# Differential heads: the gate's second part goes behind the context's row tiles, and the last row tile is turned beside it

## Chip, cores and metric

The kernel runs on one core of one Trainium2 chip. Times are microseconds of device time. TensorE (PE) multiplies and transposes, VectorE (DVE) and ScalarE (ACT) read its results, GpSimd (POOL) prepares the weights, and SyncE (SP) issues the weight loads.

## What is computed

The reference is two transformer blocks on 512 tokens. The change lies in the first layer of the second block, differential attention with eight heads over 512 tokens (four tiles of 128) and 256 context tokens (two tiles):

```python
q, k, v, z = project(h)          # and the same for the context, hc
q = apply_rope(q, cos, sin); k = apply_rope(k, cos, sin)   # tokens only
k_all = concat([k, kc]); v_all = concat([v, vc])
o1 = sweep_attention(qq[..., 0, :], kk[..., 0, :], vv)     # one softmax per half head
o2 = sweep_attention(qq[..., 1, :], kk[..., 1, :], vv)
o = rms_norm(o1 - lam * o2, subln_g) * (1 - lam_init)
return (o * silu(gate)) @ w_out
```

All of it is fp32 to the accuracy of a split: a weight `w` is kept as `w_hi` and `w_lo`, the activations likewise, and each product is three matmuls (hi by hi, lo by hi, hi by lo).

## The kernel before, in words

Each engine has its own instruction stream, written out by hand, and semaphores tie them together. The stages follow one another; `pe_heads`, `act_heads` and `dve_heads` are the stage of the differential heads.

Head `hd` is attended in twelve steps `n` (six query tiles by two half heads; `HEAD_TILES` gives the order). In each, PE makes the scores (`pe_head_scores`, into banks 0 and 1), DVE takes the extreme (`dve_head_least`), ACT the exponential (`act_head_exp`), and later PE transposes the mixed probabilities (`pe_head_at`) and multiplies by the values (`pe_head_values`). Between these steps PE fills its time with projections, in chunks of three matmuls; `HEAD_FILL` says how many chunks behind each step, 62 in all, and what is left over follows the twelfth step (`for _ in beside: pass`).

The units of this filling during head `hd` are listed by `beside_units(hd)`, each of eight chunks: six **row** units of head `hd + 1` (q, k and v of one token tile, 384 columns; tiles 0 to 3 are tokens, 4 and 5 the context) and two **z** units of head `hd` (its gate: z 0 with 512 columns, z 1 with 256). Before, the order is rows 0 to 3, z 0, z 1, row 4, row 5. Head 7 has no rows beside it. The results go into banks 5 and 6 in turn, and a unit waits until the one two before it has been read.

A row tile, once projected, is copied or rotated into `rot` (`act_head_rows` for the context, `dve_head_rows` for tokens), **turned** by four transposes on PE (`pe_head_turn`, bank 7), and read out of the bank by ACT into `q` and `k_hi` (`act_head_turned`, lines 1934 and 1935) and by DVE into `q` and `k_lo` (`dve_head_turned`, lines 2726 and 2727); the last raises `head_ready`. A turn waits for the tile's copy and for `head_ready` of the tile before. Tile `t - 1` is turned behind chunk 6 of unit `t`, tile 3 behind chunk 6 of z 0, and tile 5 at the very end of the head. The first scores of the next head wait for `head_ready` of its tile 5, and for the exponential of step 11.

The weights of head `hd` are one tile of four pairs of chunks. SP loads a pair into one of two raw buffers (four transfers of 128 KB), when POOL has split the pair two before it. POOL splits it (lines 465 and 467) into `w_hi` and `w_lo`, of which there are **two slots**: head `hd + 2` goes into the slot of head `hd`. Ahead of the first pair POOL waits for the last product that reads the slot's old tile. `product_behind` names it, and the diff leaves it as it is:

```python
if what == "head":
    return ("z", tile[1], 1)
```

PE waits for the split of a pair ahead of chunks 0, 2, 4 and 6 of a unit (`split_at`). PE's stream is in order: what stands behind a waiting chunk waits too.

Of the kernel before, what the change touches and what calls it, by code (L numbers as in the profile page):

```python
# [18 lines left out]
TX, TC = S // P, C // P  # L19
TA = TX + TC  # L20
# [455 lines left out]
def three(pe, out, a, b, start, stop):  # L476
    pe.matmul(out, a[0], b[0], start=start, stop=False)  # L477
    pe.matmul(out, a[0], b[1], start=False, stop=False)  # L478
    return pe.matmul(out, a[1], b[0], start=False, stop=stop)  # L479


def split_at(k, tile, c):

    h, v = k.sig["w_split"].at(tile)
    return h, v + c // 2
# [91 lines left out]
LAST_HALVES = {4: (0, 1), 5: (2,), 6: (3,), 7: (4,), 8: (5,), 9: (6,)}  # L577
HEAD_TILES = (0, 1, TX, TX + 1, 2, 3)
HEAD_FILL = (4, (2, 1), 6, (3, 2), 6, (3, 2), 6, (5,), 6, (5,), 6, (3, 2))
TURN_AT = 6  # L580


def head_turns(i):
# [4 lines left out]
def beside_units(hd):  # L588

    rows = [("row", hd + 1, t) for t in range(TA)] if hd < 7 else []  # L590
    return rows[0:TX] + [("z", hd, j) for j in range(2)] + rows[TX:]


def bank_order():
# [7 lines left out]
def head_bank(k, unit):  # L602
    kind, hd, t = unit
    return EARLY[t] if kind == "row" and hd == 0 and t in EARLY else 5 + k.bank_order.index(unit) % 2


def head_read(unit):

    kind, hd, t = unit
    if kind == "row":  # L610
        return [("head_v", (hd, t))] + [("head_roped", (hd, t))] * (t < TX)
    return [("head_z", (hd, t))]
# [9 lines left out]
def z_cols(j):  # L622
    return (slice(0, 512), 512) if j == 0 else (slice(512, T6), T6 - 512)
# [427 lines left out]
def tile_before(hd, t):  # L1051

    if hd == 0:
        i = FIRST_ORDER.index(t)
        return (0, FIRST_ORDER[i - 1]) if i > 0 else None
    return (hd, t - 1) if t > 0 else (hd - 1, FIRST_ORDER[-1] if hd == 1 else TA - 1)
# [35 lines left out]
def pe_head_turn(k, pe, hd, t):  # L1092

    s = k.sig
    pe.wait_ge(*s["head_roped" if t < TX else "head_plain"].at((hd, t)))
    if tile_before(hd, t) is not None:
        pe.wait_ge(*s["head_ready"].at(tile_before(hd, t)))
    for v in range(4):
        x = k.rot[:, v, :, :].rearrange("p a n -> p (a n)")
        m = pe.transpose(k.ps[:, 7, v * P:(v + 1) * P], x, k.ident[:, :])  # L1100
    m.then_inc(*s["head_turned"].up((hd, t)))


def pe_beside(k, pe, hd):

    s = k.sig
    for unit in beside_units(hd):
        kind, h, t = unit
        bank, i = head_bank(k, unit), k.bank_order.index(unit)
        if i >= 2:  # L1110
            for name, event in head_read(k.bank_order[i - 2]):
                pe.wait_ge(*s[name].at(event))
        else:
            pe.wait_ge(*s["turn_lo"].at(("h6", TX - 1, 1)))
        tile = ("head", h)
        for c in range(KD):
            if c % 2 == 0:
                pe.wait_ge(*split_at(k, tile, c))
            if kind == "row":
                m = three(pe, k.ps[:, bank, 0:384], [x[:, c, t * P:(t + 1) * P] for x in k.h6], k.hl(tile, c, 0, 384), c == 0, c == KD - 1)  # L1120
            else:
                cols, n = z_cols(t)
                m = three(pe, k.ps[:, bank, 0:n], k.hl(tile, c, 384, P), [x[:, c, cols] for x in k.h6], c == 0, c == KD - 1)
            if c == KD - 1:
                m.then_inc(*s["prod"].up(unit))
            if c == TURN_AT and kind == "row" and 0 < t != TX:
                pe_head_turn(k, pe, h, t - 1)
            if c == TURN_AT and kind == "z" and t == 0 and h < 7:
                pe_head_turn(k, pe, h + 1, TX - 1)
            yield  # L1130
    if hd < 7:
        pe_head_turn(k, pe, hd + 1, TA - 1)


def pe_head_squares(k, pe, hd):
# [53 lines left out]
def pe_heads(k, pe):  # L1189
# [3 lines left out]
    for hd in range(8):  # L1193
        beside = pe_beside(k, pe, hd)

        def fill(n):
            for _ in range(n):
                next(beside, None)
# [12 lines left out]
        for n in range(12):  # L1211
# [6 lines left out]
            elif late is None:  # L1218
                fill(sum(HEAD_FILL[n]) if n % 2 else HEAD_FILL[n])
            else:  # L1220
                for j in range(len(head_turns(late[1]))):
# [3 lines left out]
                    else:  # L1225
                        fill(HEAD_FILL[n][j])
            if n == 4 and hd > 0:
# [687 lines left out]
def act_head_rows(k, act, hd, t):  # L1915

    s = k.sig
    bank = head_bank(k, ("row", hd, t))
    act.wait_ge(*s["prod"].at(("row", hd, t)))
    if t >= TX:  # L1920
        if tile_before(hd, t) is not None:
            act.wait_ge(*s["head_turned"].at(tile_before(hd, t)))
        x = k.ps[:, bank, 0:256].rearrange("p (v o n) -> p v o n", v=4, o=1)
        act.copy(k.rot[:, :, :, :], x.to_broadcast([P, 4, 2, HD])).then_inc(*s["head_plain"].up((hd, t)))
    if hd >= 2 and t == 0:
        act.wait_ge(*s["head_valued"].at((hd - 2, 2)))
    act.copy(k.v6[:, hd % 2, t, :], k.ps[:, bank, 256:384]).then_inc(*s["head_v"].up((hd, t)))


def act_head_turned(k, act, hd, t):  # L1930
    s, b, cols = k.sig, hd % 2, slice(t * P, (t + 1) * P)
    turned = k.ps[:, 7, :].rearrange("p (v n) -> p v n", v=4)
    act.wait_ge(*s["head_turned"].at((hd, t)))
    act.activation(k.q6[0:HD, b, :, cols], turned[0:HD, 0:2, :], ACT.Copy, scale=-(HD ** -0.5))
    act.activation(k.k6[:, b, :, cols], turned[:, 2:4, :], ACT.Copy, scale=1.0).then_inc(*s["head_hi"].up((hd, t)))


def act_beside(k, act, hd):
    s = k.sig
    for unit in beside_units(hd):  # L1940
        kind, h, t = unit
        bank = head_bank(k, unit)
        for c in range(KD):
            if c == TURN_AT and kind == "row" and 0 < t != TX:
                act_head_turned(k, act, h, t - 1)
            if c == TURN_AT and kind == "z" and t == 0 and h < 7:
                act_head_turned(k, act, h + 1, TX - 1)
            if c < KD - 1:
                yield
        if kind == "row":  # L1950
            act_head_rows(k, act, h, t)
        else:
            cols, n = z_cols(t)
            act.wait_ge(*s["prod"].at(unit))
            if 0 < h < 7 and t == 0:
                act.wait_ge(*s["head_y"].at(h - 1))
            act.activation(k.z(h)[:, cols], k.ps[:, bank, 0:n], ACT.Tanh, scale=0.5).then_inc(*s["head_zth"].up((h, t)))
        yield
    if hd < 7:
        act_head_turned(k, act, hd + 1, TA - 1)  # L1960


def act_head_rstd(k, act, hd):
# [44 lines left out]
def act_heads(k, act):  # L2008
# [11 lines left out]
    for hd in range(8):  # L2020
# [6 lines left out]
        for n in range(12):  # L2027
# [10 lines left out]
            elif n % 2 == 0:  # L2038
                fill(HEAD_FILL[n])
            else:  # L2040
                fill(HEAD_FILL[n][0])
            if late is not None and len(head_turns(late[1])) > 1:
                act_head_at(k, act, *late, 1)
            if n % 2 and hd < 7:
                fill(sum(HEAD_FILL[n][1:]))
            for h in LAST_HALVES.get(n, ()) if hd == 7 else ():
# [675 lines left out]
def dve_head_turned(k, dve, hd, t):  # L2722
    s, b, cols = k.sig, hd % 2, slice(t * P, (t + 1) * P)
    turned = k.ps[:, 7, :].rearrange("p (v n) -> p v n", v=4)
    dve.wait_ge(*s["head_hi"].at((hd, t)))
    dve.scalar_tensor_tensor(k.q6[HD:P, b, :, cols], turned[HD:P, 0:2, :], -(HD ** -0.5), k.q6[0:HD, b, :, cols], ALU.mult, ALU.subtract)  # L2726
    dve.tensor_tensor(k.k6lo[:, b, :, cols], turned[:, 2:4, :], k.k6[:, b, :, cols], ALU.subtract).then_inc(*s["head_ready"].up((hd, t)))  # L2727


def dve_beside(k, dve, hd):  # L2730
    s = k.sig
    for unit in beside_units(hd):
        kind, h, t = unit
        bank = head_bank(k, unit)
        for c in range(KD):
            if c == TURN_AT and kind == "row" and 0 < t != TX:
                dve_head_turned(k, dve, h, t - 1)
            if c == TURN_AT and kind == "z" and t == 0 and h < 7:
                dve_head_turned(k, dve, h + 1, TX - 1)
            if c < KD - 1:  # L2740
                yield
        if kind == "row":
            dve_head_rows(k, dve, h, t)
        else:
            cols, n = z_cols(t)
            dve.wait_ge(*s["head_zth"].at((h, t)))
            dve.scalar_tensor_tensor(k.z(h)[:, cols], k.z(h)[:, cols], 1.0, k.ps[:, bank, 0:n], ALU.add, ALU.mult).then_inc(*s["head_z"].up((h, t)))
        yield
    if hd < 7:
        dve_head_turned(k, dve, hd + 1, TA - 1)  # L2750


def dve_head_least(k, dve, hd, n):
# [35 lines left out]
def dve_heads(k, dve):  # L2789
# [11 lines left out]
    for hd in range(8):  # L2801
# [6 lines left out]
        for n in range(12):  # L2808
# [7 lines left out]
            if hd < 7:  # L2816
                fill(sum(HEAD_FILL[n]) if n % 2 else HEAD_FILL[n])
            elif n in LAST_GATE_READ:
# [253 lines left out]
```

## Time and profile before

| | us |
|---|---|
| median of 3 runs | 1768.13 |
| the three runs | 1768.13, 1769.32, 1758.78 |
| profiled execution | 1757.89 |
| its span on the core | 1756.6 |
| PE busy in the span | 1592.8 (91%) |
| DVE busy | 1105.8 (63%) |
| POOL busy | 627.9 (36%) |
| ACT busy | 624.2 (36%) |

The profile is of one execution. A time in a row counts from the start of its span. A busy PE is not PE at its peak, because matmuls are pipelined and their recorded ends overlap the next start; the distance from one matmul's start to the next start is what it costs. "Idle before" in square brackets is time in which the engine sat still, and behind the arrow stands what released it.

### The profile page before, as it was taken

The numbers are of one execution on the slowest core, as the hardware profiler recorded it, in microseconds if no ns is written. First come the engines' busy times: TensorE is split into PE (matmuls) and PEld (weight loads), VectorE is DVE, ScalarE is ACT, GpSimd is POOL, SyncE is SP. The second block draws the span as 40 slices with busy tenths as digits, with TensorE's granted clock in tenths as the row PEclk, the third lists the DMA queues.
The fourth block names the chain that finished last, engine by engine and source line by source line (L and its number), as shares of the span: only waits on it lengthen the run. The fifth ranks groups of instructions, "written<-read, shape, count | busy, mean of one in ns | idle before, by whom it ended". The sixth has DMA issues, their size and how long they took to land. (4 is left out here: it accounts for less than half of the span.)

```text
span 1756.6 us, 21631 instructions
## 1 busy us (share of the span) xinstructions
PE 1592.8 (91%) x7933; PEld 1316.5 (75%) x7933; DVE 1105.8 (63%) x2147; ACT 624.2 (36%) x1505; POOL 627.9 (36%) x346
## 2 busy tenths in 40 slices
PE   5898889989999999988989999999997789899997
PEld 4786444777787777866778888888886568888886
DVE  6846665557777769877655655565555457665644
ACT  3213566231121210113443444444344355344431
POOL 6735000354665537644232033303323213332330
PEclk9998999999999999988989999999998989899999
DMA  5622000333443344542211011101102321111221
GB/s 175 190 68 89 1 1 1 133 102 120 138 131 115 120 158 160 185 156 86 96 49 31 19 49 49 34 16 48 49 32 65 131 73 49 49 49 29 69 85 48
DMA packets 115881, 142.55 MB, mean 81 GB/s; under 512 B 11048, under 2 KB 75200, under 8 KB 115776
## 3 DMA queue, kind: packets, MB, share of 16 engines
q1 hardware_dynamic: 89968, 91.77, 17.0%
q10 hardware_dynamic: 25808, 49.40, 8.3%
q8 instruction: 64, 1.05, 0.2%
q14 instruction: 41, 0.34, 0.1%
HBM read 132.74 MB, written 8.40 MB: 80 GB/s over the span
## 5 line engine op out<-in xcount | busy, mean ns | idle before, releaser
L465 POOL TENSOR_SCALAR w_hi<-w_raw 128x1024 fp32r<-128x1024 f32 x158 | 188.0, 1190 | 857.9 <-PE ps L479 678.7
L467 POOL TENSOR_TENSOR w_lo<-w_raw,w_hi 128x1024 fp32r<-128x1024 f32 x158 | 399.7, 2530 | 13.2
L477 PE MATMUL ps<-w_hi,h_hi 128*128 128x384 f32 (+2 forms) x768 | 285.7, 372 | 7.6 <-DVE h_lo L2266 4.4
L478 PE MATMUL ps<-w_lo,h_hi 128*128 128x384 f32 (+2 forms) x768 | 271.0, 353 | 0.0
L479 PE MATMUL ps<-w_hi,h_lo 128*128 128x384 f32 (+2 forms) x768 | 270.3, 352 | 0.0
L477 PE MATMUL ps<-h_hi,w_hi 128*128 128x512 f32 (+1 forms) x616 | 247.9, 402 | 10.3 <-POOL w_lo L467 6.3
L478 PE MATMUL ps<-h_lo,w_hi 128*128 128x512 f32 (+1 forms) x616 | 240.8, 391 | 0.0
L479 PE MATMUL ps<-h_hi,w_lo 128*128 128x512 f32 (+1 forms) x616 | 240.2, 390 | 0.0
L2487 DVE SCALAR_TENSOR_TENSOR mod_acc<-mod_piece,csil,mod_acc 128x512 f32<-128x512 f32 x140 | 190.3, 1400 | 20.9 <-DMA mod_piece<-in_ada_w 16.1
L477 PEld LDWEIGHTS ps<-w_hi,h_hi 128*128 128x128 f32 x768 | 150.2, 196 | 19.9 <-DVE h_lo L2266 4.6
L478 PEld LDWEIGHTS ps<-w_lo,h_hi 128*128 128x128 f32 x768 | 150.3, 196 | 9.8 <-issue 0.2
L479 PEld LDWEIGHTS ps<-w_hi,h_lo 128*128 128x128 f32 x768 | 149.3, 194 | 10.8
L477 PEld LDWEIGHTS ps<-h_hi,w_hi 128*128 128x128 f32 x616 | 119.1, 193 | 35.3 <-POOL w_lo L467 6.8
L479 PEld LDWEIGHTS ps<-h_hi,w_lo 128*128 128x128 f32 x616 | 118.7, 193 | 26.4
L478 PEld LDWEIGHTS ps<-h_lo,w_hi 128*128 128x128 f32 x616 | 119.2, 193 | 22.9
L2758 DVE TENSOR_REDUCE st<-ps 128x1 f32<-128x768 f32 (+1 forms) x96 | 74.6, 777 | 78.8 <-PE ps L1155 78.8
L1993 ACT ACTIVATE p<-ps,st 128x768 f32<-128x768 f32 (+1 forms) x96 | 73.1, 761 | 117.8 <-DVE st L2758 116.7
L477 PE MATMUL ps<-w_hi,g_hi 128*128 128x512 f32 x240 | 98.1, 409 | 0.2 <-POOL w_lo L467 0.2
L478 PE MATMUL ps<-w_lo,g_hi 128*128 128x512 f32 x240 | 96.3, 401 | 0.0
L479 PE MATMUL ps<-w_hi,g_lo 128*128 128x512 f32 x240 | 96.1, 400 | 0.0
L2004 ACT COPY p_turned<-ps 128x512 f32<-128x512 f32 (+1 forms) x80 | 36.5, 457 | 100.4 <-PE ps L1171 100.2
L828 PE MATMUL ps<-pt,v 128*64 128x512 f32 x108 | 59.2, 644 | 14.3 <-ACT pt L1630 14.2
(320 smaller groups left out, 2835.1 us busy)
## 6 DMA issues: line engine op xcount, KB each, us to landing
mod_piece<-in_ada_w ACTq DMA_DIRECT2D x96, 256.0 KB, 3.0
w_raw<-in_w_gate_up SPq DMA_DIRECT2D x88, 256.0 KB, 3.1
w_raw<-in_a_w_in SPq DMA_DIRECT2D x128, 128.0 KB, 2.3
w_raw<-in_w_down SPq DMA_DIRECT2D x22, 512.0 KB, 4.0
w_raw<-in_b_w_in SPq DMA_DIRECT2D x20, 512.0 KB, 3.6
w_raw<-in_w_out SPq DMA_DIRECT2D x16, 512.0 KB, 3.8
w_raw<-in_w_in SPq DMA_DIRECT2D x8, 512.0 KB, 3.8
w_raw<-in_w_o SPq DMA_DIRECT2D x8, 512.0 KB, 3.8
```

Source lines behind the costliest of these rows:

```text
L465: pool.tensor_scalar(hi, raw, 1.0, 0.0, ALU.mult, ALU.add).then_inc(*s["pool_step"].up())
L467: pool.tensor_tensor(lo, raw, hi, ALU.subtract).then_inc(*s["w_split"].up(pair))
L477: pe.matmul(out, a[0], b[0], start=start, stop=False)
L478: pe.matmul(out, a[0], b[1], start=False, stop=False)
L479: return pe.matmul(out, a[1], b[0], start=False, stop=stop)
L828: m = pe.matmul(out, k.v[:, c, v0:v0 + HD], k.pt1[:, n % 3, :], start=first, stop=last)
L1993: act.activation(folded(k.p6[:, i % 2 if sub == 0 else 2, 0:w], bs), bank_view(k, bs, P, cols), ACT.Exp, bias=f[:, sub:sub + 1], scale=-1. ...
L2004: act.copy(k.at6[:, chunks[0]:chunks[-1] + 1, (t % 2) * P:(t % 2 + 1) * P], k.ps[:, 4, 0:P * len(chunks)].rearrange("p (c n) -> p c n", n= ...
L2487: m = dve.scalar_tensor_tensor(acc, piece, w, acc, ALU.mult, ALU.add)
L2758: dve.tensor_reduce(k.st6[:, i % 4, sub:sub + 1], bank_view(k, bs, P, cols), AX.XY if len(bs) == 2 else AX.X, ALU.min).then_inc(*s["head_l ...
```

## The change

z 1 goes behind the context's row tiles: the order is rows 0 to 3, z 0, row 4, row 5, z 1. The turn of tile 5 no longer stands behind all units but behind chunk 4 of z 1; the same is done in the streams of ACT and DVE. The three copies of the rule for the turns become one function. Nothing is computed otherwise, and no instruction is added or removed.

```diff
+def turned_beside(unit, c):
+    kind, hd, t = unit
+    if kind == "row":
+        return (hd, t - 1) if c == TURN_AT and 0 < t != TX else None
+    if hd == 7:
+        return None
+    return {(0, TURN_AT): (hd + 1, TX - 1), (1, TURN_AT - 2): (hd + 1, TA - 1)}.get((t, c))

 def beside_units(hd):
     rows = [("row", hd + 1, t) for t in range(TA)] if hd < 7 else []
-    return rows[0:TX] + [("z", hd, j) for j in range(2)] + rows[TX:]
+    return rows[0:TX] + [("z", hd, 0)] + rows[TX:] + [("z", hd, 1)]

 # pe_beside; act_beside and dve_beside alike
-            if c == TURN_AT and kind == "row" and 0 < t != TX:
-                pe_head_turn(k, pe, h, t - 1)
-            if c == TURN_AT and kind == "z" and t == 0 and h < 7:
-                pe_head_turn(k, pe, h + 1, TX - 1)
+            if turned_beside(unit, c) is not None:
+                pe_head_turn(k, pe, *turned_beside(unit, c))
             yield
-    if hd < 7:
-        pe_head_turn(k, pe, hd + 1, TA - 1)
```

## Rows read from the trace of the kernel before

**Rows 1.** Windows, one per head; length, busy time of each engine, clock, DMA:

```profile
core 0: us, PE busy (x) PEld busy (x) DVE busy (x) ACT busy (x) POOL busy (x), PEclk, DMA share, GB/s
952.00:1010.50 58.50, 54.97 (x314) 51.05 (x313) 32.69 (x67) 25.47 (x61) 14.54 (x8) 0.97 0.13 37
...
1068.40:1126.40 58.00, 54.48 (x319) 50.20 (x318) 33.28 (x67) 25.77 (x61) 14.54 (x8) 1.00 0.13 37
...
1242.30:1302.50 60.20, 56.66 (x319) 52.77 (x317) 33.17 (x66) 25.82 (x61) 14.55 (x8) 0.94 0.12 36
```

**Rows 2.** Waits of PE from 949.4 to 1299.6: total, times, longest:

```profile
PE ps L1155 <- DVE k_lo L2727: 10.2, 6, 1.7
PE ps L1100 <- DVE k_lo L2727: 7.2, 6, 1.2
PE ps L1155 <- ACT p L1993: 3.8, 6, 0.6
```

**Rows 3.** Timeline of PE, end of head 2 and first steps of head 3:

```profile
1080.74 0.34 PE L479 MATMUL ps<-w_hi,h_lo 128*128 128x384 f32 x1
1082.27 0.63 PE L1100 MATMUL ps<-ident,rot 128*128 128x128 f32 x4 [1.19 <-DVE k_lo L2727]
1084.61 0.62 PE L1155 MATMUL ps<-k_hi,q 128*128 128x384 f32 x2 [1.71 <-DVE k_lo L2727]
...
1085.41 0.33 PE L477 MATMUL ps<-w_hi,h_hi 128*128 128x384 f32 x1
...
1087.33 0.34 PE L479 MATMUL ps<-w_hi,h_lo 128*128 128x384 f32 x1
1087.65 0.62 PE L1155 MATMUL ps<-k_hi,q 128*128 128x384 f32 x2
...
1088.88 0.42 PE L477 MATMUL ps<-w_hi,h_hi 128*128 128x384 f32 x1
...
1090.15 0.42 PE L477 MATMUL ps<-w_hi,h_hi 128*128 128x384 f32 x1
...
1090.76 0.56 PE L1155 MATMUL ps<-k_hi,q 128*128 128x384 f32 x2
```

**Rows 4.** Timelines of ACT and DVE in the same stretch:

```profile
1081.13 0.57 ACT L1924 COPY rot<-ps 128x512 f32<-128x512 f32 x1
```

```profile
1084.13 0.42 DVE L2727 TENSOR_TENSOR k_lo<-ps,k_hi 128x256 fp32r<-128x256 f32 x1
```

**Rows 5.** Timeline of PE, the last matmuls of z 1 of head 2:

```profile
1068.92 0.28 PE L478 MATMUL ps<-h_lo,w_hi 128*128 128x256 f32 x1
1069.04 0.28 PE L479 MATMUL ps<-h_hi,w_lo 128*128 128x256 f32 x1
```

**Rows 6.** Timeline of POOL, the split of head 4's weights:

```profile
1069.48 1.05 POOL L465 TENSOR_SCALAR w_hi<-w_raw 128x1024 fp32r<-128x1024 f32 x1 [42.73 <-PE ps L479]
1070.61 2.40 POOL L467 TENSOR_TENSOR w_lo<-w_raw,w_hi 128x1024 fp32r<-128x1024 f32 x1
1072.98 1.36 POOL L465 TENSOR_SCALAR w_hi<-w_raw 128x1024 fp32r<-128x1024 f32 x1
1074.42 2.97 POOL L467 TENSOR_TENSOR w_lo<-w_raw,w_hi 128x1024 fp32r<-128x1024 f32 x1
...
1078.49 2.38 POOL L467 TENSOR_TENSOR w_lo<-w_raw,w_hi 128x1024 fp32r<-128x1024 f32 x1
1081.23 1.05 POOL L465 TENSOR_SCALAR w_hi<-w_raw 128x1024 fp32r<-128x1024 f32 x1 [0.35 <-DMA w_raw<-in_a_w_in]
1082.36 2.34 POOL L467 TENSOR_TENSOR w_lo<-w_raw,w_hi 128x1024 fp32r<-128x1024 f32 x1
```

**Rows 7.** Timeline of DVE, the same line beside the split and away from it:

```profile
1073.46 1.68 DVE L2770 SCALAR_TENSOR_TENSOR p<-p,st 128x768 f32<-128x768 f32 x1
...
1087.39 1.02 DVE L2770 SCALAR_TENSOR_TENSOR p<-p,st 128x768 f32<-128x768 f32 x1
```

**Rows 8.** Windows of 4 us, PE alone; length, busy time, clock, DMA share, GB/s:

```profile
1256.00:1260.00 4.00, 2.22 (x9) 0.67 0.41 140
1260.00:1264.00 4.00, 4.00 (x14) 0.50 0.33 122
```

More of the change, by code:

```diff
@@ L1943, in act_beside @@
         for c in range(KD):
[L1944 to L1947, printed above, removed]
+            if turned_beside(unit, c) is not None:
+                act_head_turned(k, act, *turned_beside(unit, c))
             if c < KD - 1:
@@ L1958, in act_beside @@
         yield
-    if hd < 7:
-        act_head_turned(k, act, hd + 1, TA - 1)
 def act_head_rstd(k, act, hd):
@@ L2735, in dve_beside @@
         for c in range(KD):
[L2736 to L2739, printed above, removed]
+            if turned_beside(unit, c) is not None:
+                dve_head_turned(k, dve, *turned_beside(unit, c))
             if c < KD - 1:
@@ L2748, in dve_beside @@
         yield
-    if hd < 7:
-        dve_head_turned(k, dve, hd + 1, TA - 1)
 def dve_head_least(k, dve, hd, n):
```

## The prediction

> **What bounds the kernel now.** I first took the windows, one for each head. A head lasts 58.0 us, and PE is busy for 54.5 of them, DVE for 33, ACT for 26 and POOL for 14.5 [rows 1]. So PE sets the pace of this stage, and time is won or lost there only by what PE issues (unchanged here) and by how long it stands still.
>
> The waits of PE over six heads say where it stands still: 10.2 us ahead of the scores and 7.2 us ahead of a turn, both for DVE's `k_lo`, six times each, and 3.8 us for the exponential [rows 2]. The first two are one place, the boundary between two heads. Its timeline shows the chain: the last chunk of row 5 starts its last matmul at 1080.74 and frees PE 0.17 us later (the distance of two such matmuls, from twelve of them between 1085.41 and 1087.33), at 1080.91. The turn of tile 5 starts at 1082.27, the scores at 1084.61 [rows 3], when ACT has copied the tile and `k_lo` has been written [rows 4]. The turn itself takes PE some 0.35 us, so 1084.61 - 1080.91 - 0.35 = 3.35 us are stall. There are seven boundaries.
>
> Then I asked what else hangs on the units that are moved. POOL's timeline answers: its split of head 4's weights is released by PE, after 42.7 us of idleness, at 1069.48 [rows 6]. z 1's last matmul starts at 1069.04 and, with 0.12 us between two of its matmuls [rows 5], frees PE at 1069.16; POOL starts 0.32 us later. The four pairs are done at 1073.01, 1077.39, 1080.87 and 1084.70 [rows 6], which is 3.5, 7.9, 11.4 and 15.2 us after its start. PE wants the first pair at 1085.41 and the fourth, for chunk 6, at 1090.15 [rows 3]. The split is hidden now because z 1 ends 16 chunks before the head does, and it has only 0.7 us to spare in front of chunk 0 for the whole of it, 12.4 us for its first pair.
>
> **The change, part by part.** *The turn of tile 5 beside z 1.* Nothing is added: four transposes of 0.35 us are issued in either place. Behind the turn are now chunks 5, 6 and 7 of z 1, each three matmuls at 0.117 us, so 1.05 us of cover. From the turn's start to the scores the chain took 1084.61 - 1082.27 = 2.34 us [rows 3]. With 0.35 us of transposes and 1.05 us of chunks in it, 0.95 us of stall are left: the boundary's stall falls by 2.4 us. The bounds: a loss of nothing if ACT, which now has the exponential of step 11 right in front, makes the chain later by all of the gain; at best the full 3.35.
>
> *z 1 behind the rows.* PE's matmuls are the same; on PE alone this costs nothing, and what hides z 1's own tanh and product is PE's work on the scores. But `product_behind` still names z 1 of the old head, so POOL may start only when z 1 is done, and that is now the end of the head. What is queued behind this wait on POOL is the whole split of head `hd + 2`; behind that, on SP's queue, the loads of pairs 2 and 3; and who waits for it is PE, whose first unit of the next head is row 0 of just that tile, behind the very first scores.
>
> In the boundary's own times: without its stalls PE would be through with all chunks and the turn at 1080.91 + 0.35, say 1081.3. POOL starts at 1081.6. With the intervals of [rows 6] the pairs are split at 1085.1, 1089.5, 1093.0 and 1096.8. PE: scores at 1082.3, done in 0.8 (1085.41 - 1084.61). Chunk 0 waits from 1083.1 to 1085.2, and chunks 0 and 1 take 1.05. Chunk 2 waits until 1089.5; 2 and 3 end at 1090.6. The scores and transposes of step 1 take 1088.88 - 1087.65 = 1.2, to 1091.8. Chunk 4 waits until 1093.0, and chunk 6, the last to need a new pair, until 1096.9. From chunk 6 to the scores of step 2 are 0.61 us [rows 3], so these start at 1097.5 instead of 1090.76: 6.7 us later, the saving of 2.4 already taken off. Nothing behind gives this back, as the rest of the head is PE's own work.
>
> It happens at six boundaries (the tiles of heads 2 to 7). At the seventh, the slot goes to the output projection, whose first chunk stands only behind step 5 of head 7; there 2.4 us are gained. The sum is 6 x 6.7 - 2.4 = 37.8 us.
>
> The bounds of the split: pair 1 took 4.4 us, the others 3.5 [rows 6]. Where all four go at 3.5 us, it lasts 13.9 and not 15.2, and a boundary costs 5.4. Where all go like pair 1, it lasts 17.5 and costs 9.0. I keep 15.2, since one mix of DVE still falls beside the split (that of step 0), and since the fourth pair waited for its load even in this row.
>
> One row shows why pair 1 is slow: DVE's mix beside it took 1.68 us, and 1.02 away from the split [rows 7]; both engines lose. The Trainium skill ("GPSIMD Engine Reference", specifications) says that GpSimd's SBUF interfaces are shared with VectorE and contend with its instructions in a two-port mode or with two SBUF inputs. By that, the slow pair becomes pair 0, which has the next mix beside it, in place of pair 1, and the fourth ends at the same time.
>
> *The clock.* The end of head 5 has the same stalls as the others, but from 1256 to 1264 the granted clock is 0.67 and then 0.50, that is 1.2 GHz at the end, after PE had stood still [rows 8], and that head lasts 60.2 us and not 58.0, 2.2 more [rows 1]. The new stalls are longer (some 9 us of 15), so the fall should come more often. Much of the slow work then lies inside the waits for POOL, where it costs nothing; what counts is the part behind chunk 6. Bounds: nothing, and 2.2 at each of six boundaries, 13. I take 1.2 each, 7, less the 3 that it costs now (58.5 and 60.2 against 58.0 [rows 1], rounded up): +4.
>
> So 37.8 + 4 = 42 us. The profiled execution would go from 1757.9 to 1800. It lies 10 us below the median; of four executions shown, two lie near 1758 and two near 1769. Taken on the median, the same sum gives 1810. I forecast the middle, 1805.
>
> **The rivals.** *The quiet split.* Without PE's and DVE's traffic POOL goes at 13.9 us and the clock holds: 6 x 5.4 - 2.4 - 3 = 27, so 1785 to 1795. For it: three of four pairs are at 3.5 us. Against: the load's wait and the mix of step 0.
>
> *The clock falls at every boundary* and has not returned behind chunk 6: 6 x (6.7 + 2.2) - 2.4 - 3 = 48, so 1806 to 1816. For it: gaps of 3 us, longer than any that head 5 had. Against: four heads with the same gaps of 1.2 and 1.7 us kept the full clock, as the one at 1068.4 does [rows 1]. The Trainium skill ("TensorE: Matmul & The Clock Gate", "Why this matters for your kernels") advises against idle gaps of TensorE of this size between bursts, since they bring the half rate back; by that, this rival is the rule and my 1.2 us are too little.
>
> *The stall goes and nothing takes its place* (the other side): seven boundaries at 2.4 us each give 17 less, 1741 to 1751; at the full 3.35, 1735. It decides where the fourth pair is split before PE would want chunk 6 of the old time, 1090.1, which is 8.5 us behind POOL's start instead of 15.2. Only a tile that could be split ahead of z 1 would do that. Against it stands POOL's release by PE 0.32 us behind z 1 [rows 5, 6], in each head.
>
> *The turn is not hidden at all*, because ACT is late with it. At the six boundaries POOL's wait is later and covers it; only the seventh changes, by 2.4 us.
>
> **How the numbers follow.** Forecast 0.45, clock at every boundary 0.27, quiet split 0.20, nothing in its place 0.04, all else (a split dearer than 17.5 us, or a slot freed in another way) 0.04. The range holds the first three with the base at either end: from 1757.9 + 27, some 1786, to 1810 + 10 = 1820. A measurement of this kernel can tell about 1%, 18 us, from no change; only the case on the other side and a half-sized loss lie below that, so slower by over 1% has 0.94, and 0.03 each go to the others.
>
> **What would show it.** In the profile after: POOL's split starts within 0.5 us of z 1's last matmul, right at the boundary; PE's waits list L477 behind POOL's `w_lo` some 24 times, with 8 to 10 us per head in all; the waits for `k_lo` ahead of the turn are gone, and those ahead of the scores are near 1 us; a head lasts 64 to 67 us; PEclk is below 1 at most boundaries. I am wrong if POOL starts earlier than z 1's end, if PE's waits for `w_lo` are below 5 us per head, or if the boundary of heads 6 and 7 is not shorter.

## The result, and the profile after

| | before | after |
|---|---|---|
| median | 1768.72 (4 runs, 1758.78 to 1769.8) | 1792.16 (4 runs, 1788.52 to 1793.69) |
| ratio | | 1.0139, 95% interval 1.0106 to 1.0172 |
| span of the profiled execution | 1756.6 | 1787.2 |
| one head, in the profiled execution | 57.94, at the full clock | 64.0, mean granted clock 0.92 (window below) |

The kernel became 23.4 us slower at the median, 1.4%; the profiled execution grew by 30.6 us. The forecast of 1805 is 13 us too high, and the range of 1786 to 1820 holds the result.

The waits of PE from the end of head 0 to the end of head 6 (engine and line, what was waited for, total, times, longest) answer to [rows 2]:

```profile
PE ps L477 <- POOL w_lo L467: 37.6, 18, 2.9
PE ps L1162 <- DVE k_lo L2730: 4.2, 7, 0.6
```

The wait ahead of the turn is gone, the one ahead of the scores (L1162 now) fell from 1.7 to 0.6 us each, and a new one stands at the top: 18 waits, three for each of six heads, for POOL's split (the forecast named some 24). POOL's timeline at the end of head 3, to be held against [rows 6]:

```profile
1158.10 1.05 POOL L465 TENSOR_SCALAR w_hi<-w_raw 128x1024 fp32r<-128x1024 f32 x1 [48.58 <-PE ps L479]
1159.23 2.34 POOL L467 TENSOR_TENSOR w_lo<-w_raw,w_hi 128x1024 fp32r<-128x1024 f32 x1
1161.54 1.35 POOL L465 TENSOR_SCALAR w_hi<-w_raw 128x1024 fp32r<-128x1024 f32 x1
1162.98 2.92 POOL L467 TENSOR_TENSOR w_lo<-w_raw,w_hi 128x1024 fp32r<-128x1024 f32 x1
1166.85 1.05 POOL L465 TENSOR_SCALAR w_hi<-w_raw 128x1024 fp32r<-128x1024 f32 x1 [0.95 <-DMA w_raw<-in_a_w_in]
1167.99 2.37 POOL L467 TENSOR_TENSOR w_lo<-w_raw,w_hi 128x1024 fp32r<-128x1024 f32 x1
1170.32 1.05 POOL L465 TENSOR_SCALAR w_hi<-w_raw 128x1024 fp32r<-128x1024 f32 x1
1171.45 2.36 POOL L467 TENSOR_TENSOR w_lo<-w_raw,w_hi 128x1024 fp32r<-128x1024 f32 x1
```

And PE's timeline beside it, to be held against [rows 3]: the last matmul of z 1, the scores, and the first matmuls of chunks 0, 1, 2, 4 and 6, with the next scores.

```profile
1157.66 0.27 PE L479 MATMUL ps<-h_hi,w_lo 128*128 128x256 f32 x1
1158.53 0.62 PE L1162 MATMUL ps<-k_hi,q 128*128 128x384 f32 x2 [0.59 <-DVE k_lo L2730]
...
1161.72 0.66 PE L477 MATMUL ps<-w_hi,h_hi 128*128 128x384 f32 x1 [2.22 <-POOL w_lo L467]
...
1162.82 0.52 PE L477 MATMUL ps<-w_hi,h_hi 128*128 128x384 f32 x1
...
1165.95 0.69 PE L477 MATMUL ps<-w_hi,h_hi 128*128 128x384 f32 x1 [1.98 <-POOL w_lo L467]
...
1170.41 0.69 PE L477 MATMUL ps<-w_hi,h_hi 128*128 128x384 f32 x1
...
1173.86 0.44 PE L477 MATMUL ps<-w_hi,h_hi 128*128 128x384 f32 x1 [1.38 <-POOL w_lo L467]
...
1174.50 0.51 PE L1162 MATMUL ps<-k_hi,q 128*128 128x384 f32 x2
```

PE follows POOL pair by pair. z 1 frees PE at 1157.78, POOL starts 0.32 us later, at 1158.10, and its four pairs end at 1161.57, 1165.90, 1170.36 and 1173.81. PE starts chunks 0, 2, 4 and 6 within 0.15 us of these four times. From z 1 to the scores of step 2 it is 16.7 us. Over all six boundaries this distance is 16.18, 16.43, 16.49, 16.72, 16.24 and 16.11, and POOL's split lasts 15.18, 15.43, 15.49, 15.71, 15.24 and 15.11: the boundary is the split and 1.0 us, each time.

The windows of two heads after (columns as in [rows 1]), one behind a boundary with a split and the one over the last boundary, behind which no weights are awaited:

```profile
1056.20:1120.30 64.10, 57.59 (x318) 53.31 (x317) 33.82 (x67) 25.74 (x62) 14.41 (x8) 0.92 0.12 34
1312.10:1367.50 55.40, 53.79 (x314) 48.91 (x312) 32.68 (x62) 25.91 (x62) 15.35 (x9) 1.00 0.10 30
```

At the last boundary the change does what it says, 55.4 us against 57.9. At the six others it costs 6.1 against heads at the full clock.

### The profile page after: what moved, and what is told of

It reads as the page before. It is cut to its first block, busy times and chain, and to the rows that moved or that the text cites. A ratio compares the mean times of both kernels' runs of the same rounds, so it can differ in the third digit from the quotient of the medians.

```text
span 1787.2 us, 21631 instructions
## 1 busy us (share of the span) xinstructions
PE 1607.7 (90%) x7933; PEld 1332.2 (75%) x7933; DVE 1110.0 (62%) x2147; ACT 622.7 (35%) x1505; POOL 630.3 (35%) x346
## 3 DMA queue, kind: packets, MB, share of 16 engines
q8 instruction: 64, 1.05, 0.2%
## 4 chain that ended last, share of the span: by engine, by line
PE 63%; DVE 18%; ACT 6%; POOL 5%; issue 4%; DMA 3%; SPq 1%; ACTq 0%; DVEq 0%; POOLq 0%
PE ps L477 14%; PE ps L478 14%; PE ps L479 14%; POOL w_lo L467 3%; DVE mod_acc L2490 3%; PE ps L1192 3%; PE ps L1383 2%; PE ps L1162 2%; DVE conv_out L2490 2%; PE ps L839 2%; PE ps L1360 2%; POOL w_hi L465 1%; DMA mod_piece<-in_ada_w 1%; PE ps L869 1%; PE ps L820 1%
## 5 line engine op out<-in xcount | busy, mean ns | idle before, releaser
L477 PE MATMUL ps<-w_hi,h_hi 128*128 128x384 f32 (+2 forms) x768 | 289.6, 377 | 45.0 <-POOL w_lo L467 37.6
```

## The experiments

In the table a head's length is the distance between two starts of DVE's gate product (`dve_head_gate`, once a head), read from one profiled execution of each kernel; before, these starts are at 984.95, 1042.91, 1100.85 and so on, to 1336.33. The first five lengths hold the boundaries behind heads 1 to 5, each with a split behind it, and the sixth holds the last, between heads 6 and 7; the boundary between heads 0 and 1 lies ahead of them.

| kernel | median, us | ratio to before | six head lengths, us |
|---|---|---|---|
| before | 1768.7 | | 57.96, 57.94, 57.94, 57.93, 60.28, 59.33 |
| after | 1792.2 | 1.0139 | 64.02, 64.09, 64.29, 63.83, 63.69, 55.45 |
| cols_after | 1741.4 | 0.9845 (0.9812 to 0.9877) | 55.76, 55.93, 55.75, 56.55, 55.31, 55.44 |
| cols_before | 1767.7 | 1.0000 (0.9975 to 1.0024) | 59.26, 60.60, 59.29, 60.52, 59.25, 60.42 |
| z1_mid | 1764.8 | 0.9995 (0.9974 to 1.0017) | 59.73, 59.23, 59.84, 59.23, 59.84, 58.69 |
| z1_last_turn_end | 1796.4 | 1.0150 (1.0107 to 1.0193) | 63.52, 62.91, 65.54, 64.79, 64.84, 57.30 |
| short_split | 1768.3 | 1.0018 (0.9991 to 1.0045) | 60.07, 59.28, 60.98, 59.36, 60.70, 55.39 |
| cols_early | 1748.7 | 0.9896 (0.9869 to 0.9924) | 58.18, 58.18, 58.17, 55.91, 55.30, 55.38 |
| early_fill5 | 1740.0 | 0.9849 (0.9813 to 0.9885) | 55.76, 55.77, 55.92, 56.35, 55.31, 55.38 |
| early_fill6 | 1744.4 | 0.9876 (0.9844 to 0.9907) | 55.91, 55.90, 55.75, 56.47, 55.30, 55.39 |

Each ratio is to runs of the kernel before on the same chip: the medians of these are 1766.1 for cols_after, cols_before, z1_mid and z1_last_turn_end, and 1766.2 for short_split, cols_early and the two below it. My theory was the forecast's: the new order lets POOL begin the split only at the boundary, and PE waits for it. The rivals: the order of the units costs something of its own (banks, reads), the split counts whenever it is later, or the turn's saving is independent of POOL.

### The wait taken away: cols_after

The slot of a head's weights is released in two steps. Its q, k and v columns have all been read by the end of the head before; only the z columns are still to be read, by z 0 and z 1. So the tile is loaded and split in two parts, each with its own release:

```diff
 # not shown: SP's load of head_z, PE's waits for it, and the release of the slots for out0
 # list_weights: columns 0 to 383 in four pairs, the z columns of all eight chunks as one part of 1024
-            w.append((("head", hd), [... for j in range(4)], 0, KD))
+            w.append((("head", hd), [... for j in range(3)], 0, KD))
+            w.append((("head_z", hd), [(0, P, a_in[:, hd * P + 3 * D:hd * P + 3 * D + P])], 0, KD))
 # product_behind
-        return ("z", tile[1], 1)
+        return ("row", tile[1], last_tile(tile[1]))
 # pool_program, for the part head_z of head h
+            if h >= 2:
+                pool.wait_ge(*s["prod"].at(("z", h - 2, 1)))
```

> Edit: the changed kernel, but the weights of a head are loaded and split as two parts: q, k and v columns in four pairs, which wait only for the last row tile that read the slot, and the z columns of all eight chunks in one part of the same size, which waits for z 1 of two heads before. Theory (the loss is PE's wait for a split that z 1 holds back): PE's waits for w_lo in the heads vanish, a head lasts 54.5 to 55.5 us, the time is 15 to 25 us below the kernel before, near 1745. Rival (the loss comes from the order of the units itself, its banks or reads): the time stays near the changed kernel's 1790.

It is 24.8 us faster than before on the same chip and some 51 us faster than the change as it stands, at the far end of the 15 to 25 us that were expected. Its waits of PE from 965 to 1295, complete:

```profile
PE ps L1204 <- DVE p L2795: 5.9, 6, 1.1
PE ps L1188 <- DVE k_lo L2756: 3.6, 6, 0.6
PE ps L1135 <- DVE rot L2738: 0.5, 1, 0.5
```

No wait for a split is left, with the same order of units and the same turn. So no cost of the order itself shows, and the loss was POOL's release. A head lasts 55.8 us at the full clock, a little over the 54.5 to 55.5 that were expected:

```profile
1042.70:1098.60 55.90, 54.25 (x319) 50.40 (x318) 35.01 (x67) 25.67 (x62) 15.64 (x10) 1.00 0.13 39
```

### The tool without the change: cols_before

The same split by columns in the kernel before.

> Edit: the kernel before, with the same split by columns. Theory: nothing waits for the split there, so the time is that of before within 3 us, and the stall at the boundary of the heads is as it was (1.2 and 1.7 us). Rival (the split by columns is a gain of its own, so that cols_after says nothing on z 1): it is faster than before by more than 5 us.

A ratio of 1.0000, and PE's waits at the boundaries are the same 10.2 and 7.2 us as in [rows 2]: where the split was hidden, releasing it earlier gives nothing. The gain of cols_after is that of the change, once its price is gone.

### Half the way: z1_mid

```diff
-    return rows[0:TX] + [("z", hd, j) for j in range(2)] + rows[TX:]
+    return rows[0:TX] + [("z", hd, 0)] + rows[TX:TX + 1] + [("z", hd, 1)] + rows[TX + 1:]
```

> Edit: the kernel before, with z 1 between row 4 and row 5, and the turn of tile 5 at the end. The split of the next but one head starts 4.2 us later. Theory (a threshold: the fourth pair has some 5.4 us to spare ahead of chunk 6): the time is that of before within 4 us, and PE waits for w_lo nowhere in the heads or under 0.5 us. Rival (every microsecond by which the split starts later counts, through the loads or the traffic): 4 us in each of six heads, 20 to 25 us slower.

No difference, and no wait for `w_lo` in the heads. The first and the last instruction of POOL's split, and the next two of PE's matmuls that open a chunk (the second is chunk 6):

```profile
1076.10 1.05 POOL L465 TENSOR_SCALAR w_hi<-w_raw 128x1024 fp32r<-128x1024 f32 x1 [44.74 <-PE ps L479]
...
1088.88 2.64 POOL L467 TENSOR_TENSOR w_lo<-w_raw,w_hi 128x1024 fp32r<-128x1024 f32 x1
```

```profile
1093.41 0.34 PE L477 MATMUL ps<-w_hi,h_hi 128*128 128x384 f32 x1
1094.08 0.42 PE L477 MATMUL ps<-w_hi,h_hi 128*128 128x384 f32 x1
```

The split starts 10.4 us before the boundary's scores (1086.54) where it was 15.1 before (1084.61 - 1069.48), and ends at 1091.5, still 2.6 us ahead of chunk 6. So the price has a threshold: 4.7 us later is free, and the 14.7 us of the change (from 15.1 ahead of the scores to 0.4) are not. Where between them it begins was not run; the 5.4 us that the fourth pair had to spare ahead of chunk 6 are an estimate of it.

### The split made shorter: short_split

```diff
-            pool.tensor_tensor(lo, raw, hi, ALU.subtract)
+            pool.tensor_scalar(lo, raw, 2.0 ** -12, 0.0, ALU.mult, ALU.add)   # heads 2 to 7 only
```

> Edit: the changed kernel, but for heads 2 to 7 POOL writes w_lo with a one-input instruction (the raw weight times 2 to the power of -12, in 1.05 us) in place of the two-input subtraction (2.35 us); so w_lo of these heads isn't the low part of the split, and the rest is as it was. A pair then takes 2.2 us of POOL, and the load of pairs 2 and 3 (3.8 us behind the split before) sets their pace: the fourth pair is done some 10 us behind z 1's end, not 15.4. Theory: each of six boundaries gets 5 us shorter, 1760 to 1768, and waits for w_lo fall from 6.2 to 1 or 2 us a head. Rival (the split's length is not what counts, but that it starts late): 1785 to 1792.

1768.3, a ratio of 1.0018: with a split of 10.6 to 12.4 us, the changed kernel takes as long as the one before. So the split's length sets the loss, and not only its late start. The waits of PE for `w_lo` are 21.1 us over six heads, not 37.6; that is 3.5 a head, more than the 1 or 2 that were expected:

```profile
PE ps L480 <- POOL w_lo L468: 21.1, 23, 1.2
PE ps L1165 <- DVE k_lo L2733: 4.1, 7, 0.6
```

A head became 3 to 5 us shorter and not 5 throughout, and at each of the six boundaries POOL's third pair now waits for its load, 1.4 to 2.9 us; here 2.4:

```profile
1041.40 1.05 POOL L465 TENSOR_SCALAR w_hi<-w_raw 128x1024 fp32r<-128x1024 f32 x1 [2.40 <-DMA w_raw<-in_a_w_in]
```

### The turn put back: z1_last_turn_end

The changed order, with the turn of tile 5 behind z 1 at the very end.

> Edit: the changed kernel with the turn of tile 5 at the end again, behind z 1, so only the order of the units is changed. Theory (POOL's wait covers the turn at six boundaries): the same as the changed kernel or up to 4 us slower, the last boundary giving 2 us of it. Rival (the turn beside z 1 saves 2.4 us at each boundary whatever POOL does): 15 to 20 us slower than the changed kernel, near 1808.

Its median is 4.3 us above that of the change, at the end of what was expected, and the two ratios to before (1.0150 and 1.0139) have intervals that overlap, so the two kernels are not told apart; the rival's 15 to 20 us are ruled out. The turn's saving is covered by the wait at six boundaries. At the last one, where nothing covers it, both profiles are at the full clock and show it: 57.30 us with the turn at the end, 55.45 with the turn beside z 1. In the profiled execution of this kernel the stall for `k_lo` came back (9.8 us, six times) and the wait for `w_lo` fell by as much (27.2, against 37.6). But the head lengths do not agree with each other, 62.9 and 65.5. The windows of these two:

```profile
1056.60:1119.50 62.90, 56.97 (x318) 52.39 (x317) 34.73 (x66) 25.75 (x62) 14.16 (x8) 0.95 0.12 34
1119.50:1185.10 65.60, 59.69 (x318) 54.75 (x317) 34.77 (x67) 25.83 (x63) 13.73 (x8) 0.90 0.11 33
```

In the longer one PE was still at the low clock when the last pair came, which its matmuls of chunk 6 show:

```profile
1172.54 0.69 PE L477 MATMUL ps<-w_hi,h_hi 128*128 128x384 f32 x1 [0.75 <-POOL w_lo L467]
1173.02 0.52 PE L478 MATMUL ps<-w_lo,h_hi 128*128 128x384 f32 x1
1173.34 0.52 PE L479 MATMUL ps<-w_hi,h_lo 128*128 128x384 f32 x1
```

The last two stand 0.32 us apart, where 0.17 is the full clock. In the head of 62.9 us the clock had come back by chunk 6:

```profile
1108.86 0.45 PE L477 MATMUL ps<-w_hi,h_hi 128*128 128x384 f32 x1 [1.92 <-POOL w_lo L467]
```

From there to the next product of the gate it is 10.6 us, and 12.6 in the longer head (1172.54 to 1185.1). So 2.0 of the 2.6 us between the two heads lie behind the last wait, which is where a low clock costs time here.

### What is left in cols_after: cols_early, early_fill5, early_fill6

cols_early turns tile 5 behind chunk 3 of z 1, not 4:

> Edit: cols_after with tile 5 turned behind chunk 3 of z 1, not chunk 4. Theory (0.59 us of wait for k_lo are left ahead of the scores because the cover of three chunks is too short): that wait goes at seven boundaries, 2 to 4 us faster than cols_after, 1737 to 1740. Rival (ACT's exponential and copies are in the way, so the turn's reading doesn't come earlier): no difference.

The wait for `k_lo` went, and the wait for the mix of probabilities took its place, 1.65 us in one piece:

```profile
1022.40 0.79 PE L1204 MATMUL ps<-ident,p 128*128 128x128 f32 x4 [1.65 <-DVE p L2795]
```

Behind it the clock was down in three of six heads (58.2 us instead of 55.9), and the median is 7 us above cols_after, where 2 to 4 us less were expected. The other two move a chunk, or two, ahead of that wait (`HEAD_FILL` begins with 5, (1, 1) or with 6, (1, 0)).

> Edit: cols_early with five chunks behind step 0 and one and one in step 1 (before: four, then two and one). In cols_after PE waits 1.07 us in step 1 of each head for the mix of the head before. Theory: a chunk of 0.52 us moved ahead of it takes half of this wait, 3 to 4 us faster than cols_early. Rival (the chain through the scores moves along with it): no difference.

> Edit: cols_early with six chunks behind step 0 and one and none in step 1. Theory: the wait for the mix goes, but with one chunk between the transposes and nothing behind them the scores of step 2 may wait for the exponential; from 2 us faster to 3 us slower than early_fill5.

early_fill5 came out 8.7 us below cols_early, and early_fill6 4.4 above early_fill5, both outside what was expected. These are medians of four and six runs. So cols_after, cols_early and early_fill5 were run again on one chip.

> The kernel of cols_after once more, on one chip with the next two. The first traces put it at 55.8 us a head with the full clock. Theory (the wait for k_lo is real but short, and the clock's chance at the boundary makes up the rest): 1738 to 1744.

> The kernel of cols_early once more. Its trace showed the wait for k_lo moved into the wait for the mix, 1.65 us in one piece in place of 0.6 and 1.1, and the clock down in three of six heads. Theory (one longer wait in a place with few matmuls tips the clock): 4 to 8 us slower than cols_after. Rival (chance of the first executions): within 2 us of it.

> The kernel of early_fill5 once more. Theory (a chunk moved ahead of the mix makes the one wait 1.1 us again): as cols_after or up to 3 us faster.

Medians on one chip: 1742.2 (1739.95 to 1744.44), 1746.5 (1742.29 to 1754.1) and 1742.0 (1737.85 to 1744.71); their ratios to before, 0.9875, 0.9906 and 0.9874. This time the profiled execution of cols_early had all heads at 56.0 us, so its three slow heads were no fixed property. That execution took 1746.0, though, and the first one, with three slow heads, 1742.0: these heads do not decide the time of an execution by themselves. Turning earlier is no gain. early_fill5 equals cols_after within the measurement, and the interval of cols_early overlaps theirs. early_fill6, not repeated, is not told apart from them. cols_after is faster than the kernel before by 1.55% on one chip and 1.25% on the other, and so faster than the change too.

## Why the prediction was right, and where its terms were off

**The chain of the argument held at each link.** POOL starts 0.32 us behind z 1, in each head. Its split takes 15.1 to 15.7 us, where 15.2 was taken from [rows 6]. PE waits ahead of chunks 0, 2 and 6 of the next head. There are six such boundaries, and the seventh is shorter: 55.45 us, where the heads of before at the full clock have 57.94. That these 2.5 are near the 2.4 taken for the turn is partly luck. z1_last_turn_end has 57.30 at this boundary, so the turn's new place is worth 1.9 us, and the other 0.6 (57.94 - 57.30) are as long as the exponential's wait, which the new order removes. cols_after shows by experiment what the forecast only argued, that this release is the loss. It also is the rival of the other side made true, but its 1741.4 meets that rival's 1741 by chance: the rival counted 17 us from the fast profiled execution, and cols_after gained 24.8 at the median.

**A boundary cost 6.1 us and not 6.7.** From z 1 to the scores of step 2 it was 16.1 to 16.7 us, 16.4 in the mean, near the 16.2 of the forecast (1081.3 to 1097.5). Before it was 9.5 (1081.3 to 1090.76), so this stretch cost 6.9, and the rest of the head gave some of it back, which the forecast had ruled out: it is 47.6 us in every head, where it was 57.94 - 9.5 = 48.4. 0.6 of these 0.8 us are a wait that I had read and left alone, the 3.8 us over six heads for the exponential [rows 2]. It stood behind z 1's short chunks, and with the longer chunks of row 4 in their place it is gone from the list. The other 0.2 stay unexplained.

**The clock's term had the wrong sign.** I took +1.2 us at each of six boundaries, less 3 us for the cost of the clock in the kernel before, together +4. The clock did fall, at every one of the six boundaries with a split. One of them (windows of 4 us, PE alone, columns as in [rows 8]):

```profile
1156.00:1160.00 4.00, 2.91 (x21) 1.00 0.00 0
1160.00:1164.00 4.00, 2.26 (x6) 0.67 0.23 66
1164.00:1168.00 4.00, 2.05 (x6) 0.50 0.45 127
1168.00:1172.00 4.00, 3.97 (x15) 0.55 0.35 102
1172.00:1176.00 4.00, 2.62 (x15) 1.00 0.57 165
```

It was back ahead of chunk 6. The slow matmuls filled time that POOL's split takes anyway: the wait ahead of chunk 4, which I had at 1.2 us, is not in the list (at this boundary it was 0.4 at most: the transposes and what stands idle behind them take 1.09 us up to chunk 4, and 0.70 at the boundary behind head 2), and the one ahead of chunk 2 is 2.0 and not 3.3. That the boundary is the split and 1.0 us at all six says the same: no cost of the clock is left in it. For the same reason PE's waits for `w_lo` are 6.3 us a head, while I had named 8 to 10, and below 5 as what would refute me. A wait and a slow clock in one place did not add up here; the later of the two decided. So the term should have been nothing in the changed kernel, less what the clock cost in the profile of before. The rival in which the clock costs 2.2 at each boundary falls in this kernel, but z1_last_turn_end shows its mechanism at work, with 2 us a head, where the clock fell later against the last pair. The rule of the Trainium skill that I had put beside it ("TensorE: Matmul & The Clock Gate", "Why this matters for your kernels") is borne out in what it says of the clock: at this boundary the trace has 0.50 behind waits of 2.2 and 2.0 us. It says nothing of whether that lies on the path.

**Where the 13 us come from.** The sum said 42 us for the profiled execution, and it grew by 30.6. The boundaries account for 3.7 of the difference: 6 x 6.1 - 2.5 = 34.1, not 37.8. Most of the rest is the clock's term, +4 where some -5 came out. From the first scores of the first head to the last gate product the two executions are 29.3 us apart, 34.1 less 4.8. The new kernel paid nothing for its falls, and the profile of before had falls at three of its seven boundaries, the last of them (59.33 us) not counted in my 3. Another 2.0 us come up ahead of the heads (first scores at 913.3, not 911.3), where the two kernels are the same. The 5 us that I put on top for the distance to the median were about right: the changed kernel's median is 3.6 above its profiled execution.

**The base.** The medians differ by only 23.4. The kernel before was at the full clock in four of the six heads listed, and in the profiled execution of cols_before, which is equal to it in time, no head is shorter than 59.2. One of these:

```profile
1044.90:1105.50 60.60, 55.74 (x318) 51.63 (x317) 34.51 (x67) 25.74 (x62) 14.91 (x10) 0.97 0.12 36
```

Against such heads, 59.9 us in the mean, the change costs 4.1 at a boundary and gains 4.4 at the last (59.9 - 55.45), and 6 x 4.1 - 4.4 = 20, nearer the 23.4 than 34 is. That the other executions of the kernel before look like cols_before is inferred from their times and not seen; only one was profiled.

The measured 1792 lies in the interval of the quiet split, 1785 to 1795, and not by its reason: the split was no shorter than 15.1 us, where that rival wanted 13.9, and the clock did not hold.

The slow pair stayed pair 1, at 4.3 us, in the changed kernel, though I had written that it becomes pair 0. DVE's mix starts at 1160.60, some 2.5 us behind POOL's start, and lies mostly beside pair 1's instructions; pair 0 took 3.5 us. The fourth pair ended 15.7 us behind POOL's start here and 15.1 to 15.5 at the other five boundaries, near the 15.2 that I had kept.

## What to carry to other kernels

Before moving the last reader of a buffer, find what waits for that read: a piece of code that names the last reader for a whole tile makes every later use of the slot hang on it, and the engine that then starts late may be one that looked idle two thirds of the time. Measure its slack to the point of need. A move within it is free (4.7 us here); beyond it the whole stretch lasts as long as the late work does (the split and 1.0 us here, 6 us more a head). Where only some columns of the buffer are read late, release the others earlier; here this turned 1.4% of loss into 1.25 to 1.55% of gain. Before summing a change on a single profiled execution, see how far that execution is from the median, and do not add a slow clock to a wait that covers it.

## What the runs showed of the hardware

The granted clock fell to 1.2 GHz behind two stalls of PE of 1.2 and 1.7 us (0.50 in [rows 8]), and not behind the same two stalls at four boundaries in a row of the same execution. A head is 57.94 us without the fall and 59.2 to 60.6 where the clock fell (before and cols_before), 1.3 to 2.7 us more. What decides whether it comes, no run here shows. Removing a short stall of PE can be worth more than its length: cols_after, whose stalls at the boundary are 0.6 and 1.1 us, has the full clock in all six heads, and these are 55.8 us where those of cols_before are 59.9. That is 4.1 us a head, of which 2.1 are there at the full clock too (57.94 - 55.8).

The times of one kernel spread, and these heads are not the whole of it. The kernel before had 1759.26 to 1775.33 in 19 runs on one chip, cols_after 1739.29 to 1742.8 in 4, but early_fill5, whose heads are as long as those of cols_after, 1733.14 to 1746.01 in 4. And two executions of the same kernel came to the first scores of the first head 10.4 us apart, cols_early and its repeat:

```profile
908.23 0.98 PE L1188 MATMUL ps<-k_hi,q 128*128 128x384 f32 x2 [1.68 <-issue]
```

```profile
918.58 0.98 PE L1188 MATMUL ps<-k_hi,q 128*128 128x384 f32 x2 [1.68 <-issue]
```

So stages ahead of the heads vary by as much as the heads do; what varies there was not looked into.

POOL and DVE were slower when both worked. At each of the six boundaries of the changed kernel DVE's product by a scalar took 1.36 to 1.41 us where it began beside POOL's subtraction, and 0.68 away from the split:

```profile
1160.60 1.39 DVE L2767 TENSOR_SCALAR p<-p,st,lam 128x768 f32<-128x768 f32 x1
```

```profile
1150.56 0.68 DVE L2767 TENSOR_SCALAR p<-p,st,lam 128x768 f32<-128x768 f32 x1
```

How much it loses depends on when it begins. In the kernel before it began 0.3 us ahead of the subtraction's end (1073.01, [rows 6]), not 1.0, and took 0.73:

```profile
1072.69 0.73 DVE L2768 TENSOR_SCALAR p<-p,st,lam 128x768 f32<-128x768 f32 x1
```

In both it ends 0.4 us behind the end of POOL's subtraction, at 1073.42 and at 1161.99, as if it had waited for it; the rows show no more than these times. POOL loses too, in pair 1 of both kernels: 1.35 us and not 1.05 for its copy, 2.92 to 2.97 and not 2.35 for its subtraction.
